# Other banks for the down sums, late modulations one up tile later, and the forget columns as stationary operand

## What is computed

```python
sc = silu(c); mod = sc @ w_mod[layer] + b_mod[layer]        # 1024 -> 6 x 1024
shift1, scale1, gate1, shift2, scale2, gate2 = split(mod, 6)
h = rmsnorm(x, g_attn) * (1 + scale1) + shift1
proj = h @ w_in[layer]                # 3078 columns: q, k, v of heads A, B, C, and 6 forget columns fz
oa = diff_attention(rope(qa), rope(ka), va, lam)
ob = dilated_mixture_attention(rope(qb), rope(kb), vb)
oc = forgetting_attention(qc, kc, vc, cumsum(log_sigmoid(fz + forget_bias)))
x = x + gate1 * (concat(oa, ob, oc) @ w_out)
h = rmsnorm(x, g_mlp) * (1 + scale2) + shift2
u, g = split(h @ w_up, 2)             # 2 x 2816 columns
x = x + gate2 * ((silu(causal_conv3(g)) * u) @ w_down)
```

## Time and profile before

| | |
|---|---|
| median of 3 runs (2060.54 to 2062.87) | 2062.0 us |
| profiled execution | 2056.69 us |
| its span, first to last instruction | 2054.9 us |
| TensorE busy in matmuls | 1661.8 us, 81% |
| VectorE, ScalarE, GpSimd busy | 517.9, 292.4, 64.8 us |
| mean rate of DMA | 292 GB/s |
| granted TensorE clock, mean | 0.906 |
| chain that ended last | TensorE 59%, DMA 36% |

### The profile page before, as it was taken

How to read it: one execution, slowest core, us unless ns; L and a number is a source line. 1 busy time by engine, 2 the same in 40 slices (tenths; PEclk the granted TensorE clock), 3 DMA queues, 4 the chain that set the end, 5 groups by cost and what they waited for, 6 DMA issues and landing times.

```text
span 2054.9 us, 19503 instructions
## 1 busy us (share of the span) xinstructions
PE 1661.8 (81%) x8176; PEld 883.9 (43%) x8176; DVE 517.9 (25%) x1222; ACT 292.4 (14%) x787; POOL 64.8 (3%) x68
## 2 busy tenths in 40 slices
PE   7999999999999999999856566655999765665665
PEld 3566888444568874457312121211466211121211
DVE  1673556312334220244201010100164110010101
ACT  1142000011420000125201000000234100010000
POOL 0000000000000000031000000000120000000000
PEclk9999999999999999999988787887999877787868
DMA  9891788646226440655699999999943999999997
GB/s 364 281 330 54 256 306 303 224 131 201 97 81 217 164 144 33 192 182 205 270 421 421 422 422 422 422 422 421 319 162 144 369 421 421 421 422 422 422 422 315
DMA packets 184327, 599.56 MB, mean 292 GB/s; under 512 B 18752, under 2 KB 77760, under 8 KB 135104
## 3 DMA queue, kind: packets, MB, share of 16 engines
q1 hardware_dynamic: 184014, 598.03, 75.5%
q10 hardware_dynamic: 242, 0.53, 0.1%
HBM read 594.75 MB, written 3.80 MB: 291 GB/s over the span
## 4 chain that ended last, share of the span: by engine, by line
PE 59%; DMA 36%; DVE 3%; ACT 2%; issue 1%; POOL 0%; DVEq 0%; SPq 0%; ACTq 0%; POOLq 0%
PE ps L981 14%; DMA extra<-in_w_down 13%; DMA extra<-in_w_up 12%; DMA extra<-in_w_gate 10%; PE ps L764 9%; PE ps L1010 8%; PE ps L1289 7%; PE ps L1051 6%; PE ps L1189 3%; PE ps L926 3%; PE ps L862 1%; PE ps L657 1%; PE ps L679 1%; PE ps L845 1%; DVE extra L1914 1%
## 5 line engine op out<-in xcount | busy, mean ns | idle before, releaser
L1289 PE MATMUL ps<-ring,wide 128*32 128x512 f32 x2240 | 346.6, 775 | 220.2 <-DMA ring<-in_w_down 91.6
L981 PE MATMUL ps<-hT,ring 128*128 128x256 f32 (+1 forms) x1664 | 310.8, 349 | 0.0
L981 PEld LDWEIGHTS ps<-hT,ring 128*128 128x128 f32 x1664 | 277.8, 192 | 34.4 <-issue 4.6
L1289 PEld LDWEIGHTS ps<-ring,wide 128*32 128x32 f32 x2240 | 82.9, 137 | 466.2 <-issue 220.1
L1289 PE MATMUL ps<-extra,wide 128*32 128x512 f32 x784 | 139.2, 845 | 93.8 <-DMA extra<-in_w_down 35.3
L764 PE MATMUL ps<-ring,hT 128*128 128x512 f32 (+1 forms) x448 | 177.3, 552 | 2.0 <-ACT hT L1369 2.0
L1010 PE MATMUL ps<-ring,wide 128*128 128x512 f32 x352 | 157.1, 608 | 7.9 <-DVE wide L2159 7.9
L2475 DVE TENSOR_TENSOR wide<-ps,wide 128x512 f32<-128x512 f32 x16 | 10.3, 686 | 512.5 <-PE ps L1289 512.5
L1051 PE MATMUL ps<-ring,hT 128*128 128x512 f32 (+2 forms) x320 | 127.3, 555 | 0.3 <-issue 0.3
L764 PEld LDWEIGHTS ps<-ring,hT 128*128 128x128 f32 x448 | 80.6, 193 | 92.5 <-issue 90.5
L1289 PEld LDWEIGHTS ps<-extra,wide 128*32 128x32 f32 x784 | 32.0, 148 | 199.2 <-issue 84.9
(11 more groups left out here) (271 smaller groups left out, 1398.2 us busy)
## 6 DMA issues: line engine op xcount, KB each, us to landing
ring<-in_w_gate SPq DMA_DIRECT2D x24, 4096.0 KB, 34.3
ring<-in_w_down SPq DMA_DIRECT2D x24, 4096.0 KB, 33.7
ring<-in_w_up SPq DMA_DIRECT2D x22, 4096.0 KB, 33.3
ring<-in_w_mod SPq DMA_DIRECT2D x24, 2048.0 KB, 12.6
ring<-in_w_up SPq DMA_DIRECT2D x44, 1024.0 KB, 7.9
extra<-in_w_gate SPq DMA_DIRECT2D x8, 4096.0 KB, 34.3
extra<-in_w_up SPq DMA_DIRECT2D x8, 4096.0 KB, 33.3
extra<-in_w_down SPq DMA_DIRECT2D x8, 4096.0 KB, 33.9
```

What stands on the lines that cost most here:

```text
L981: last = mm(ps[2 * (j % 2) + half][:, f * T + o:f * T + o + n], wt[:, k, w:w + P], h8[:, k, o:o + n], start=k == 0, stop=k == KD - 1)
L1289: last = mm(ps[bank + n][e * CAP:(e + 1) * CAP, :], lhs[:, k, e * CAP:(e + 1) * CAP], expert_at(n0, e, k % PAIR, n * N), start=k == 0, sto ...
```

## The change

Three edits in the first block, and small ones that come with them.

- Down sums lie in banks 6, 7, 2, 3. TensorE waits before `down` for `product(9)` only. In layer 1 the wait for the last product stands before the first modulation of the down stage, in layer 2 before the last two tiles.
- Late modulations come one up tile later (`LAG = 2`): none behind `up(1)`, the first behind `up(2)`, and in layer 1 three in the down stage instead of two. The tile list follows.
- The six forget columns are no tile. They are loaded for both layers at the start into `fgate`, ahead of `rows` and the gate biases on SyncE's queue. After position 2 `gate_sums` multiplies them as stationary side in four column groups of 32 against all 256 tokens, ScalarE copies the result, and `gate_fold` adds up the groups. Flips, sums and modulations of positions 3 to 6 move to the same projection tile under its new position.
- Modulations 8 and 9 use banks 0 and 1, so `score1(1)` waits for their output. GpSimd clears one more strip (26 columns), and the clears share a semaphore, of which ScalarE waits for all four before its first instruction. In the second block `score` waits for `att_max_ready`. VectorE waits for all three loads that count on `rows_loaded`.

The diff without its counts, semaphore names and start-up waits:

```diff
@@ -19,7 +19,7 @@
-IN1 = 3078
+IN1 = 3072
@@ -35,7 +35,6 @@
-B1_F = 3072
@@ -46,14 +45,17 @@
-IN1_ORDER = (0, 1, 2, 6, 3, 4, 5)
-MOD_AT = {4: (4, 5), 5: (6, 7), 6: (8, 9)}
-SUM_AT = {1: (4,), 3: (5,), 5: (6, 7), 6: (8, 9)}
-FLIPS_AT = {3: (0, 1), 4: (2, 3), 5: (4,), 6: (5, 6)}
+IN1_ORDER = (0, 1, 2, 3, 4, 5)
+LAST_IN = 5
+MOD_AT = {3: (4, 5), 4: (6, 7), 5: (8, 9)}
+SUM_AT = {1: (4,), 3: (5,), 4: (6, 7), 5: (8, 9)}
+FLIPS_AT = {2: (0, 1), 3: (2, 3), 4: (4,), 5: (5, 6)}
...
+LAG = 2
+DOWN_BANK = (6, 7, 2, 3)
@@ -73,8 +75,8 @@
-            if 1 <= n <= len(late):
-                tiles.append((late[n - 1][0], "mod", late[n - 1][1]))
+            if LAG <= n < len(late) + LAG:
+                tiles.append((late[n - LAG][0], "mod", late[n - LAG][1]))
@@ -232,6 +234,7 @@
+        fgate = sb("fgate", [P, DEPTH * KD * CH + 32 - CH])
@@ -509,6 +513,9 @@
+            for l in range(DEPTH):
+                sp.dma_start(fgate[:, l * KD * CH:(l + 1) * KD * CH].rearrange("p (k n) -> p k n", k=KD),
+                             a["w_in"][l, :, IN1:IN1 + CH].rearrange("(k p) n -> p k n", p=P)).then_inc(sems["rows_loaded"], 16)
@@ -651,7 +658,7 @@
-                    pe.wait_ge(*s.at("att_scores_read", m - 1))
+                    pe.wait_ge(*s.at("att_max_ready", m - 1))
@@ -712,7 +719,7 @@
-                    b = (0 if done else 2 if L == 0 and q in MOD_AT[6] else 4) + q % 2
+                    b = (0 if done else 0 if L == 0 and q in MOD_AT[LAST_IN] else 4) + q % 2
@@ -810,6 +817,23 @@
+                def gate_sums():
+                    pe.wait_ge(sems["rows_loaded"], 48)
+                    pe.wait_ge(sems["pads_cleared"], 4)
+                    for k in range(KD):
+                        o, w = 32 * (k % 4), (L * KD + k) * CH
+                        last = mm(ps[5][o:o + 32, 0:T], fgate[:, w:w + 32], h8[:, k, :], start=k < 4, stop=k >= 4)
+                    last.then_inc(s.up("b1_gate_done"), 1)
+                def gate_fold():
+                    pe.wait_ge(*s.at("b1_gate_read", 1))
+                    for c in range(2):
+                        last = mm(ps[5][:, T + CH * c:T + CH * (c + 1)], fsum[:, c * P:(c + 1) * P], tb("fold")[:, 0:CH],
+                                  start=True, stop=True)
+                    last.then_inc(s.up("b1_gate_folded"), 1)
@@ -876,7 +900,7 @@
-                        if i == 6:
+                        if i == LAST_IN:
@@ -890,29 +914,33 @@
-                        if i == 6:
+                        if i == LAST_IN:
...
-                    if i == 6:
-                        pe.wait_ge(*s.at("b1_proj_by_act", 6))
-                        pe.wait_ge(*s.at("b1_proj_by_dve", 6))
+                    if i == 2:
+                        gate_sums()
+                    if i == LAST_IN:
+                        pe.wait_ge(*s.at("b1_proj_by_act", 5))
+                        pe.wait_ge(*s.at("b1_proj_by_dve", 5))
...
-                    if i == 3:
+                    if i == 2:
...
-                    if i in (3, 4):
-                        pe.wait_ge(*s.at("b1_rotated", i - 2))
+                    if i in (2, 3):
+                        pe.wait_ge(*s.at("b1_rotated", i - 1))
...
-                pe.wait_ge(*s.at("b1_proj_by_act", 7))
-                pe.wait_ge(*s.at("b1_proj_by_dve", 7))
+                    if i == 2:
+                        gate_fold()
+                pe.wait_ge(*s.at("b1_proj_by_act", 6))
+                pe.wait_ge(*s.at("b1_proj_by_dve", 6))
...
-                score1(1)
...
+                score1(1)
@@ -995,19 +1023,17 @@
-                modulation(EARLY[L])
...
-                    if j <= late:
-                        modulation(EARLY[L] + j - 1)
-                pe.wait_ge(*s.at("b1_product_ready", UPT))
-                pe.wait_ge(*s.at("b1_mod_ready", min(EARLY[L] + UPT - 1, len(MODS[L]))))
+                    if j - LAG < late:
+                        modulation(EARLY[L] + j - LAG)
+                pe.wait_ge(*s.at("b1_product_ready", UPT - 1))
...
-                    return mm(ps[4 + 2 * c + n][:, :], prod[:, f, c * P:(c + 1) * P],
+                    return mm(ps[DOWN_BANK[2 * c + n]][:, :], prod[:, f, c * P:(c + 1) * P],
@@ -1017,8 +1043,10 @@
-                    if UPT + j <= late:
-                        modulation(EARLY[L] + UPT + j - 1)
+                    if UPT + j - LAG < late:
+                        pe.wait_ge(*s.at("b1_product_ready", UPT))
+                        modulation(EARLY[L] + UPT + j - LAG)
+                pe.wait_ge(*s.at("b1_product_ready", UPT))
@@ -1334,10 +1362,10 @@
-            act.wait_ge(sems["rpb_clear"], 1)
+            act.wait_ge(sems["pads_cleared"], 4)
...
-            act.wait_ge(sems["ssm_clear"], 1)
+            act.wait_ge(sems["pads_cleared"], 4)
@@ -1436,12 +1464,15 @@
-                    if i == 4:
+                    if i == 2:
+                        act.wait_ge(*s.at("b1_gate_done", 1))
+                        av(fsum, ps[5][:, 0:T], ACT.Copy).then_inc(s.up("b1_gate_read"), 1)
+                    if i == 3:
...
-                    if i == 6:
+                    if i == LAST_IN:
@@ -1917,7 +1949,7 @@
-                    b = (0 if t > B1_AT[(L, "down", 0)] else 2 if L == 0 and q in MOD_AT[6] else 4) + q % 2
+                    b = (0 if t > B1_AT[(L, "down", 0)] else 0 if L == 0 and q in MOD_AT[LAST_IN] else 4) + q % 2
@@ -2081,13 +2113,10 @@
-                    if i == 3:
-
-                        dve.wait_ge(*s.at("b1_proj_by_act", 4))
+                        dve.wait_ge(*s.at("b1_gate_folded", 1))
...
-                        dve.wait_ge(*s.own())
-                        tt(f3, proj1[:, :, B1_F:B1_F + 6], fb, ALU.add).then_inc(s.up(), 1)
+                        tt(f3, ps[5][:, T:T + 2 * CH].rearrange("p (c h) -> p c h", c=2), fb, ALU.add).then_inc(s.up(), 1)
@@ -2164,12 +2193,12 @@
-                    if 1 <= j <= late:
-                        mod_out(EARLY[L] + j - 1)
+                    if LAG <= j < late + LAG:
+                        mod_out(EARLY[L] + j - LAG)
...
-                for j in range(UPT, late + 1):
-                    mod_out(EARLY[L] + j - 1)
+                for j in range(UPT, late + LAG):
+                    mod_out(EARLY[L] + j - LAG)
@@ -2181,7 +2210,7 @@
-                    residual(4 + 2 * c + n, c, n, 1, "b1_mlp_added", 2 * c + n)
+                    residual(DOWN_BANK[2 * c + n], c, n, 1, "b1_mlp_added", 2 * c + n)
@@ -2320,9 +2349,9 @@
-                            .then_inc(s.up("att_scores_read"), 1)
+                            .then_inc(s.up(), 1)
...
-                        ts(dst, src, mp["scale"], None, ALU.mult).then_inc(s.up("att_scores_read"), 1)
+                        ts(dst, src, mp["scale"], None, ALU.mult).then_inc(s.up(), 1)
```

More of the change, by code:

```diff
@@ L181 @@
 SHARED_COUNT = {
-    "dve_step": (243, 131, 89, 89), "act_step": (25, 25, 38, 38), "pool_step": (2, 2, 11, 9),
+    "dve_step": (243, 131, 101, 101), "act_step": (25, 25, 38, 38), "pool_step": (2, 2, 11, 9),
     **{"att_" + name: (n, n, MAPS2, MAPS2) for name, n in (
-        ("scores_done", NP1), ("scores_read", 0), ("max_ready", 2 * NP1), ("probs_ready", 2 * NP1),
+        ("scores_done", NP1), ("max_ready", 2 * NP1), ("probs_ready", 2 * NP1),
         ("probs_flipped", 2 * NP1), ("probsT_ready", NP1), ("values_done", NP1), ("out_read", NP1))},
@@ L187 @@
 COUNTS = {**B1_COUNT, **STREAM_COUNT, **B2_COUNT, **G_COUNT, **SHARED_COUNT}
-ONCE = ("cols_loaded", "x_loaded", "first_tab_loaded", "b1_head_loaded0", "b1_head_loaded1", "b1_head_loaded2", "tab_loaded", "rows_loaded", "gate_bias", "csil", "rpb_clear", "rpb_loaded",
-        "ssm_clear", "rpb_copied", "gain_loaded", "router_loaded", "router_padded", "fin_gain", "fin_sumsq", "fin_mean", "fin_rstd", "fin_scaled", "out_stored")
+ONCE = ("cols_loaded", "x_loaded", "first_tab_loaded", "b1_head_loaded0", "b1_head_loaded1", "b1_head_loaded2", "tab_loaded", "rows_loaded", "gate_bias", "csil", "rpb_loaded",
+        "rpb_copied", "gain_loaded", "router_loaded", "pads_cleared", "fin_gain", "fin_sumsq", "fin_mean", "fin_rstd", "fin_scaled", "out_stored")
 MISCOUNT = []
@@ L246, in two_blocks @@
         sm = spare[:, 0:1536].rearrange("p (a n) -> p a n", a=3)
+        fsum = spare[:, 1536:1536 + T]
         pT = spare[:, 1536:2560].rearrange("p (a n) -> p a n", a=2)
@@ L1247, in _ @@
                 pe.wait_ge(sems["router_loaded"], 16)
-                pe.wait_ge(sems["router_padded"], 1)
+                pe.wait_ge(sems["pads_cleared"], 4)
                 route(0)
@@ L1738, in inv_root @@
                 gt(dst[:, 0:n], tmp[:, 0:n], tb("half")[:, 0:n], ALU.pow).then_inc(s.up(name), 1)
-            gp.memset(rpad[:, :], 0.0).then_inc(sems["rpb_clear"], 1)
-            gp.memset(router[:, DEPTH * KD * EXP:(DEPTH * KD + 1) * EXP], 0.0).then_inc(sems["router_padded"], 1)
+            gp.memset(rpad[:, :], 0.0).then_inc(sems["pads_cleared"], 1)
```

(6 more changed lines are left out.)

## The result

The changed kernel runs at a median of 2053.9 us (2049.9 to 2055.2) against 2062.0 (2056.6 to 2064.7) for the kernel before: ratio 0.9958, 95% interval 0.9939 to 0.9977. A repeat in another set gave 0.9952 (0.9939 to 0.9966). So the change gains some 8 to 10 us, clear of noise though only 0.4 to 0.5%. The forecast was 26.8 us and 2035.2, and its range ended at 2044. The direction was right, the size was not, and the true time lies outside the range.

The account below looks back on a forecast made before the run. First block bound by TensorE with stalls, experts by DMA. Savings 4.8 + 4.8 + 6.0 + 6.7 + 2.1 + 2.4 = 26.8 us give 2029.9 profiled; plus 5.3 to the median, 2035.2 us, range 2030 to 2044.

Parts of the forecast that it names:

- Late modulations and down sums: First block's up and down tiles: removed TensorE stalls save 4.8 + 6.0 us in layer 1, 4.8 + 6.7 in layer 2.
- The rival of a starved ring (C): Up-tile steps: mixed transfers fall to 220 GB/s, steps last 19 us, kernel slower at 2074 us; chance 0.03.
- that of a new wait in the up tiles (B): Up tiles: later-requested modulation tiles arrive late or the clock falls elsewhere; gain 12 to 20, time 2046 us; chance 0.09.
- that of gaps that come back (D): Removed stalls return one by one because something not shown is as late; 2058 to 2062 us; chance 0.04.
- Forget columns, layer 2: `gate_sums` and fold before layer 2's flips: column groups cut 3.5 us to 0.9 + 0.4, saving 2.1 us.
- Forget columns, layer 1: Start of layer 1: flips 1.3 us earlier and 1.1 us of slow clock saved, together 2.4 us.
- the term x: Layer 1's start: delay of modulation tile 4 by the added forget load, between 0 and 4.1 us, taken as 1.
- nearest to the dip: A forget load among other transfers shows 183 GB/s against 410, about 1 us lost; basis for the delay taken.
- Rival A: Start: forget loads delay it by 4.1 us and the clock falls anyway; gain 20.8, time 2041 us; chance 0.13.
- the 1.1 us that was forecast: Behind layer 1's flips: the clock no longer falls, so 32 records take 13.8 us instead of 14.92.
- a term put at nothing: Ring: without the six-column tile every later tile is requested one tile earlier, listed among parts that cost nothing.
- the new wait of `score`: Second block's attention: score waits for the maximum of m-2; taken as 0, or 0.3 us twice if cover failed.

Follow-up runs that it names:

- repeat: The changed kernel run once more unaltered, beside the kernel before: 2052.0 us, ratio 0.9952.
- the repeated kernel before: The kernel before run once more unaltered: 2059.4 us from a single run.
- both repairs: Changed kernel with late forget loads and four empty ring places behind layer 2's up tiles 5 to 8 (list of 78): 2028.1 us, ratio 0.9824.
- both, placed: Version with late forget loads and 78-place list, plus unused columns putting ring and `extra` at multiples of 512 B: 2020.3 us, ratio 0.9808.
- both loads late: Changed kernel with layer 1's forget load behind modulation tile 4's request, layer 2's behind the router's load; with nothing else changed, 2039.2 us, ratio 0.9886.
- its padding undone: Changed kernel with one empty ring place behind each layer's third projection tile, so the list is 76 long again: 2039.5 us, ratio 0.9889.
- its buffers moved by 32 B: Changed kernel with an unused tensor of 8 columns ahead of the last two large buffers: ratio 0.9964.
- the forget part alone: Changed kernel with late modulations (LAG = 1), down-sum banks and waits as in the kernel before: 2082.0 us, ratio 1.0092.
- the late version moved by 32 B: Changed kernel with both layers' forget loads issued later, plus 8 unused columns ahead of the last two large buffers: ratio 0.9926.
- the late modulations and down sums alone: Kernel before with LAG = 2, the new down-sum banks and the shifted product wait, nothing of the forget columns: 2046.4 us, ratio 0.9908.

## Why the prediction was right and wrong

Time gained against the kernel before, by stage, each from starts in the traces (the repeat against the repeated kernel before):

| stage | predicted | after | repeat | both repairs | both, placed |
|---|---|---|---|---|---|
| to the first flips of layer 1 | 1.3 | -4.1 | -4.3 | 2.8 | 3.1 |
| flips to the first up tile | 1.1 | -5.0 | -2.1 | 1.2 | -3.6 |
| up and down of layer 1 | 10.8 | 10.9 | 13.1 | 10.9 | 10.9 |
| projections and attention of layer 2 | 2.1 | 1.9 | 1.9 | 1.9 | 1.9 |
| layer 2's up tiles to the second block's second tile | 11.5 | 1.6 | 1.9 | 12.0 | 12.0 |
| from there to the end | 0 | -3.8 | -3.1 | 4.6 | 12.0 |
| sum | 26.8 | 1.5 | 7.4 | 33.4 | 36.3 |

**Late modulations and down sums: right.** 10.8 was forecast for layer 1 and measured at 10.9 in three of four executions (the 13.1 has 2.2 of scatter in the kernel before, whose stage took 251.7 and 253.8 us in two executions). 11.5 was forecast for layer 2 and 12.0 measured where the way into the second block is free. Adding the idle time, the slow clock behind it and the shortened instruction, each from its own row, was a method good to half a microsecond. The rival of a starved ring (C), that of a new wait in the up tiles (B) and that of gaps that come back (D) did not come: none of the rows between 213 and 367 us shows a wait.

**Forget columns, layer 2: right** (2.1 and 1.9), the column groups included.

**Forget columns, layer 1: the failed step is the term x.** It was bounded by 0 and 4.1, from one such load alone on the queue, and taken as 1, "nearest to the dip". The transfer came 6.4 us later than before. The count was right, one load more than before ahead of tile 4, but two things were wrong. x was the price of the added load alone, though the old one moved too, from behind the rows and gates to ahead of them: there the first costs 2.4 us (66.10 against 63.67), in its old place it had cost no more than 0.5 (64.22, and 63.7 to 63.9 in the other three profiles with it there), and the second costs 4.5, above the bound. And the dip to 183 GB/s was read as the whole price of a load, though it was one load with large pieces on either side; with two in a row, which also hold SyncE's next large request back from 43.73 to 49.19 us, the engines ran dry, as the windows at 19 to 83 GB/s show. With the flips late, the clock fell too, and the next 32 records took 15.67 us (15.85 in the repeat), where they take 13.84 in the versions with both loads late. Behind the flips another 2.1 us were lost in the repeat. Rival A described this case (x at its bound, the clock falling anyway) and held it at 0.13 with a gain of 20.8. Its mechanism is the one that came, at half of the real price: it took 4.2 us off this place (3.1 and 1.1), and the repeat shows 8.8 (-4.3 - 2.1 against 1.3 + 1.1). The sentence of the Trainium skill that stood beside it (DMA: Bandwidth & Descriptors, "Specifications", at least 512 B a piece) pointed the right way; what is measured is above what was worked out from it. With the loads moved behind tile 4 and both repairs, the place gained 2.8 where x = 0 gives 2.3 (0.5, 2.2 and 3.1 in the other three such kernels), and the 32 records behind the flips took 13.84 us instead of 14.92 in all four, the 1.1 us that was forecast. That the whole stage gained 1.2 in one of them is luck: it took 120.2, 120.2 and 121.9 us in the others.

**The way into the second block: the second failed step, a term put at nothing.** The prediction said: "The six-column tile leaves the ring, so every later tile is requested one tile earlier." That holds within the first block, whose list shifts. It fails at its end, since the list is rounded up: two real places became empty ones that count as used last. It cost 10.5 us, shown twice (76 and 78 places, with and without the late loads). The arithmetic stood in the code: 74 rounded up to 78 leaves four of the six places that the next block's tiles stand behind. The other parts put at nothing held where a row shows them: in the second block's second layer, from its first projection tile to the first expert matmul, the changed kernel with its padding undone takes 154.7 us and the kernel before 154.6, so the new wait of `score` costs nothing (the changed kernel itself takes 155.5, which belongs to the open point below).

**To the end: one open point.** The last stage took 1203.3 and 1203.2 us in the changed kernel, 1203.3 with its buffers moved by 32 B and 1202.6 in the forget part alone, against 1199.5 and 1200.1 in the kernel before, 1198.9 with the padding undone, 1200.6 in the late version moved by 32 B and 1201.0 with the late modulations and down sums alone. The traces say where most of it lies: from the first projection tile of the second block's second layer to its last expert matmul the first four take 596.4 us (596.3 to 596.5) and the other five 593.9 to 594.3. What the four share and the others don't is two loads at the start together with a list of 74. What makes these 2.4 us was not found, and no run tested it.

**The scatter was underrated.** The prediction allowed 1 to 2 us. In the attention the clock falls in some executions and not in others: layer 1's stage took 117.0 to 124.4 us over all kernels (118.1 and 118.2 in two executions of the kernel before), and layer 2's projections and attention took 5 to 6 us more in three of the fourteen profiles than the 155.0 (with the forget part) or 156.9 (without) of the rest. The 15 runs of the kernel before in the last set spread over 2058.1 to 2065.2 us.

## What to carry to other kernels

When an operation leaves a ring or a queue, follow the count that frees its places to the next user, with the rounding at the end: what goes out in the middle may come back as a wait at the boundary. Price a load in small pieces with all such loads ahead of the first large one that is needed, and with what it holds up in the issuing queue: here the second cost more than the first, and a load cost more ahead of the tables than behind them. It belongs behind the last transfer that anyone waits for. In a stage bound by transfers, look at where the destination begins: here 24 unused columns were worth 0.2%, half of what the whole change brought.

## What the hardware showed that was not expected

Transfers to SBUF of 8 KB pieces ran at 422 GB/s with ring and `extra` off a multiple of 512 B a partition, at 424 with `extra` on it, and at 427 to 428 with both on it; packets in the trace took 314.4, 312 and 309.1 ns on average. 2048 pieces of 24 B kept the rest of a queue at 19 to 83 GB/s for 6 us. And 16 records of 32 columns in four column groups took 1.00 us, with no visible price for changing the tiling before and behind them.
